# The selected branch's gate moved from the prologue of the last phase into the pair that uses it

## The reference, cut to what matters

```
q, z, gl = split(h @ w_in)                         # z: three gate paths, one per branch
o_cmp = attend(q, 32 compressed keys)
o_sel = attend(q, top-16 blocks of 64 keys)
o_win = attend(q, the last 512 keys)
mix = sum over branches of sigmoid(gl) * o * silu(z)
x = x + gate * (mix @ w_out)
```

## Time and profile before

| | us |
|---|---|
| median of 3 runs | 1825.84 (1825.52 to 1826.37) |
| the profiled execution | 1824.16 |
| its span, first to last instruction | 1822.5 |
| TensorE busy | 1652.4 (91%) |
| VectorE busy | 898.5 (49%) |
| ScalarE busy | 585.5 (32%) |
| GpSimd busy | 500.7 (27%) |

### The profile page before, as it was taken

How to read it: one execution, slowest core, us unless ns; L and a number is a source line. 1 busy time by engine, 2 the same in 40 slices (tenths; PEclk the granted TensorE clock), 3 DMA queues, 4 the chain that set the end, 5 groups by cost and what they waited for, 6 DMA issues and landing times.

```text
span 1822.5 us, 32217 instructions
## 1 busy us (share of the span) xinstructions
PE 1652.4 (91%) x11976; PEld 1464.4 (80%) x11976; DVE 898.5 (49%) x2338; ACT 585.5 (32%) x1310; POOL 500.7 (27%) x305
## 2 busy tenths in 40 slices
PE   3799999996995979789999999999999999998987
PEld 0688888885995977588988888888898888876877
DVE  1444454556226141155555655556555565567345
ACT  2423333432005040023424344243442433434112
POOL 0131322117431332363011110111101111039462
PEclk8899999998998988889999999999999999998998
DMA  9123222333331242301021130211110111133822
GB/s 355 36 93 126 98 100 99 103 130 113 110 117 39 90 143 78 105 24 33 16 59 33 27 79 22 75 33 27 33 27 25 33 27 33 28 96 90 267 84 105
DMA packets 81581, 146.17 MB, mean 80 GB/s; under 512 B 19058, under 2 KB 52882, under 8 KB 81266
## 3 DMA queue, kind: packets, MB, share of 16 engines
q1 hardware_dynamic: 68202, 129.69, 22.1%
q10 hardware_dynamic: 10288, 8.46, 1.5%
q0 software_dynamic: 2944, 6.04, 1.2%
HBM read 130.01 MB, written 19.35 MB: 82 GB/s over the span
## 4 chain that ended last, share of the span: by engine, by line
PE 82%; DVE 7%; ACT 4%; issue 3%; DMA 2%; ACTq 0%; POOL 0%; SPq 0%; DVEq 0%
PE PS L902 15%; PE PS L904 14%; PE PS L903 14%; PE PS L1149 10%; PE PS L1162 9%; PE PS L1129 4%; PE PS L1130 4%; PE PS L1242 3%; ACT XT L1345 2%; ACT HT_r L1348 1%; PE PS L1139 1%; PE PS L1094 1%; PE PS L933 1%; PE PS L1158 1%; DMA KD<-w_bo 1%
## 5 line engine op out<-in xcount | busy, mean ns | idle before, releaser
L902 PE MATMUL PS<-HT_r,WR_r 128*128 128x344 f32 x1368 | 467.5, 342 | 58.6 <-DVE WR L1657 27.6
L904 PE MATMUL PS<-HT_r,WR_r 128*128 128x344 f32 x1368 | 449.3, 328 | 0.0
L903 PE MATMUL PS<-XT_r,WR_r 128*128 128x344 f32 x1368 | 448.7, 328 | 0.0
L594 POOL TENSOR_TENSOR WR_r<-WR,ONE 128x1024 fp32r<-128x1024 f32 x65 | 126.9, 1952 | 1100.9 <-DMA WR<-w_b 650.9
L902 PEld LDWEIGHTS PS<-HT_r,WR_r 128*128 128x128 f32 x1368 | 268.8, 196 | 66.1 <-DVE WR L1657 31.0
L1424 ACT ACTIVATE PB<-PB,NM 128x257 f32<-128x257 f32 (+9 forms) x384 | 249.0, 650 | 178.3 <-DVE NM L1791 178.0
L903 PEld LDWEIGHTS PS<-XT_r,WR_r 128*128 128x128 f32 x1368 | 268.8, 196 | 0.4
L904 PEld LDWEIGHTS PS<-HT_r,WR_r 128*128 128x128 f32 x1368 | 267.7, 196 | 0.0
L1149 PE MATMUL PS<-CST,PB 128*128 128x128 f32 (+1 forms) x1360 | 226.0, 285 | 2.4 <-ACT PB L1420 1.2
L1804 DVE COPY PT<-PS 128x256 f32<-128x256 f32 (+2 forms) x192 | 121.7, 634 | 201.3 <-PE PS L1149 200.5
L1162 PE MATMUL PS<-PT,VT 128*64 128x128 f32 x2592 | 204.0, 285 | 6.5 <-DVE SS L1844 2.8
(11 more groups left out here) (283 smaller groups left out, 2373.1 us busy)
## 6 DMA issues: line engine op xcount, KB each, us to landing
WR<-w_ada SPq DMA_DIRECT2D x64, 512.0 KB, 5.4
WR<-w_b SPq DMA_DIRECT2D x32, 512.0 KB, 3.4
WR<-w_a SPq DMA_DIRECT2D x17, 512.0 KB, 5.0
STR<-scratch SPq DMA_DIRECT2D x128, 48.0 KB, 1.9
KD<-w_bo SPq DMA_DIRECT2D x9, 512.0 KB, 3.7
XT<-x SPq DMA_DIRECT2D x8, 516.0 KB, 15.2
HT<-x SPq DMA_DIRECT2D x8, 516.0 KB, 4.5
x_mid<-HT SPq DMA_DIRECT2D x8, 516.0 KB, 6.1
```

The source lines that it names most:

```text
L594: pool.tensor_tensor(high_r, raw, ONE[:, 0:1].unsqueeze(2).to_broadcast([P, NC, P]), ALU.mult).then_inc(sem("w_split"), 1)
L902: pe.matmul(out, hw[:, k, :], high, start=(k == 0), stop=False)
L903: pe.matmul(out, hw[:, k, :], low, start=False, stop=False)
L904: return pe.matmul(out, lw[:, k, :], high, start=False, stop=(k == NC - 1))
```

## The change

The selected branch's gate leaves the prologue (three thirds fewer there) and is computed in units 0 to 2 of the pair that uses it, where the sliding branch's was. The sliding branch's goes to units 3 to 6, the next pair's queries to units 7 to 10, and the next pair's compressed gate to units 11 to 16. The last pair, which has no next one, now holds six thirds instead of three. The chunks of the weights are numbered and loaded to suit, the query third's last bank is 3 instead of 6, and a wait on an evicted third of the prologue goes.

```diff
-N_Q0, N_AO, N_KV, N_GL, N_B0, N_B, N_BO = 2, 18, 26, 32, 33, 36, 65
+N_Q0, N_AO, N_KV, N_GL, N_B0, N_B, N_BO = 2, 18, 26, 32, 33, 35, 65
...
             prologue.append(third_fill("q", None, 0, a, N_B0 + 1))
-        for a in range(3):
-            prologue.append(third_fill("gate", "sel", 0, a, N_B0 + 2))
         for it in range(PAIRS):
...
-            kinds = [("gate", "win", it, n), ("q", None, it + 1, n + 1), ("gate", "cmp", it + 1, n + 2), ("gate", "sel", it + 1, n + 3)]
+            kinds = [("gate", "sel", it, n), ("gate", "win", it, n + 1), ("q", None, it + 1, n + 2), ("gate", "cmp", it + 1, n + 3)]
             if it == PAIRS - 1:
-                spans = spans[0:3]
+                spans = spans[0:6]
...
-                fl["bank"] = (0, 1, 2, 7)[i] if ph == "a" else (4, 5, 6, 0, 1, 6, 2, 3, 7)[i]
+                fl["bank"] = (0, 1, 2, 7)[i] if ph == "a" else (4, 5, 6, 0, 1, 3)[i]
...
-            weights(N_B0 + 2, t["w_b"][2])
-            weights(N_B, t["w_b"][3])
+            weights(N_B, t["w_b"][2])
+            weights(N_B + 1, t["w_b"][3])
...
-                weights(n + 1, t["w_b"][4 * it + 4])
-                weights(n + 2, t["w_b"][4 * it + 5])
+                weights(n + 2, t["w_b"][4 * it + 4])
+                weights(n + 3, t["w_b"][4 * it + 5])
...
-                weights(n + 3, t["w_b"][4 * it + 6])
...
-                weights(n + 4, t["w_b"][4 * it + 7])
+                weights(n + 4, t["w_b"][4 * it + 6])
...
+                weights(n + 5, t["w_b"][4 * it + 7])
...
-                    pe.wait_ge(*evicted(pl["prologue"][7]))
...
-                    for fl in pl["prologue"][6:9]:
-                        third_out(fl)
```

## The result

| | before | changed |
|---|---|---|
| median of the runs, us | 1825.68 (1818.56 to 1826.37, 4 runs) | 1843.14 (1835.92 to 1847.28, 4 runs) |
| ratio to before, 95% interval | | 1.0101 (1.0072 to 1.0130) |
| the profiled execution, us | 1824.16 | 1839.88 |
| its span, us | 1822.5 | 1838.2 |

The changed kernel is slower by some 18 us (13 to 24 by the interval). The forecast was 1849, with a range of 1832 to 1855. The direction and the larger part of the sum came out as forecast. The first step, on the prologue, did not: there the change gains. The interval is 0.3% to either side, wider than the 0.2% that the prediction allows for.

What follows compares the result with a forecast made beforehand. GpSimd was taken to bound both the prologue's end and the last pair. Start +1.5, closing list +20.5 and clock +1.5 gave +23.5 on 1824.16, 1847.7; against the runs' median the forecast was 1849, range 1832 to 1855.

Steps and rivals of the forecast that it cites:

- The first step: Prologue: taking the gate's thirds off TensorE buys nothing; the start of the pairs' steady part moves by +1.5 us.
- The closing list: Last pair: GpSimd's 66.6 us list begins 24.54 later behind the last third, so the scores come 20.5 us later.
- Rivals 2 and 3: 2: closing list has unseen slack, TensorE's arrival decides, 1837, chance 0.06; 3: GpSimd waited for in neither place, 1820, chance 0.04.
- The clock behind the waits: Behind the waits at the end: TensorE comes out cold, costing +1.5 us, with bounds 0 and 4.4.
- The pairs: Pairs 0 to 6: twelve thirds each at the same units, only rotated, costed at 0.
- rival 4: Pairs: the rotation costs a wait in each of seven pairs, 12.6 us more, 1862; chance 0.05.
- The start of the pairs: Prologue into pair 0: the start of the pairs' steady part moves by +1.5 us.
- the walk turn by turn: Prologue: VectorE's 13 operations alternate one for one with GpSimd's 14, ending at 808.3 against 802.62, before the softmax.
- The prediction's other end for the six copies: Prologue: if the copies into the compressed keys don't wait, VectorE reaches the softmax at 802.6, a move of about -1.
- Rival 1: Prologue: the turns don't bind and the pairs start 15.5 us earlier, the closing list staying late, 1832; chance 0.14.

Runs made afterwards that it cites:

- Run 3: Kernel before, with only GpSimd's closing list made to wait for the softmax of the selected branch's last unit in the last pair: 1.0092 of before, 1843.37 us.
- run 2: Changed kernel with a shorter GpSimd closing list: output and weight splits first, then 20 of 48 value pages, SyncE issuing the other 28: 1.0070 of before.
- run 1: Changed kernel with the split of chunk 36 put ahead of GpSimd's key splits again: 1.0075 of before.
- run 5: Kernel before with the short closing list (output and weight splits first, 20 value pages on GpSimd, 28 on SyncE): 0.9989 of before.
- run 7: Both kernels with short closing list and key splits moved behind the pairs' third and fourth chunks and into pair 1: 0.9963 (before), 1.0020 (changed) of before.

## Why the prediction was right, and where it was not

**The closing list: right, in mechanism and in size.** Rivals 2 and 3, in which nothing waits for the list, are ruled out by the 9.39 and 0.81 that TensorE stood for it. The prediction has 9.9 for the three thirds, 24.54 for the later start of the list, 66.6 for its length and +20.5 for the scores. Measured from the first transpose of pair 7 to the scores: 110.07 less 89.31, +20.8. The thirds cost 10.1 (44.92 less 34.84). The list began 32.70 behind the second transpose of pair 7 (1640.77 less 1608.07) and not 8.17 as before (1620.49 less 1612.32): 24.53 later. Run 3 shows that the lateness of the list alone is enough (ratio 1.0092), run 2 that without it TensorE does not wait.

**The clock behind the waits: too large.** It was put at +1.5 on top. TensorE did come out of the wait slow: the granted clock of the stretch behind it is 0.50, which is 1.2 GHz, and the next is at 2.4 GHz throughout (lengths and busy times as in the earlier trace rows).

```profile
1701.00:1705.40 4.40, 4.36 (x15) 4.39 (x16) 0.00 (x0) 0.00 (x0) 4.38 (x9) 0.50 0.38 107
1705.60:1712.00 6.40, 5.59 (x59) 2.68 (x58) 0.00 (x0) 0.00 (x0) 6.17 (x6) 1.00 0.04 10
```

But this passed while it would have waited for the half split anyway, as one sentence of that step allowed; from the scores to the end nothing was lost (-0.8; the stretch lies between 128.9 and 131.8 in the eleven profiles). Its lower bound, 0, was the answer.

**The pairs: nothing for the rotation, right.** D has the same mean in both orders, to some 4 us with this scatter, and rival 4 (12.6 more) is ruled out by it.

**The start of the pairs: wrong in sign.** The forecast was +1.5, measured -4.4 (B). The step that failed is the walk turn by turn, "one for one they end at 808.3". It laid all of VectorE's 13 operations against GpSimd's 14 and let each wait for a whole one. The trace shows three things that the walk left out.
- The turns are not one for one. A GpSimd operation comes 0.08 behind the last. A VectorE copy of 0.17 that was waiting ends before that, and the next one right behind it begins ahead of GpSimd again: of the four copies at 773.47 two took 0.18, of the two query copies one took 0.17. The longer operations did wait in turn, save one of the four query splits, which took 0.69 because GpSimd was idle then for the 1.03 of chunk 36.
- What waits early costs nothing. The six copies lost 6.7 (8.10 against 1.36 in run 1), but VectorE had idle time after them, until ScalarE had the queries' high parts: 8.91 before, still 3.52 in the changed kernel. The walk added their waits to the path. Of what grew, only the query splits, 4.9 longer, were on it.
- What left had been on the path. Before, the query copies were over at 793.95 and the softmax began at 802.62: the 8.7 between them went to the SiLUs of the three thirds that leave and the copy behind these. In the changed kernel the softmax follows the query copies at once. So the 11.0 that leave TensorE did buy something, 7.3 in B with the key splits where they were (run 1).

Put together, the softmax came 8.4 earlier after the first third than the walk has it, and the way from there to the first transpose took 2.7 longer than its 5.0, because GpSimd, which the walk has idle by then, was not; from the first transpose to the second 11.83 came for 12.0. The two errors partly cancel. The prediction's other end for the six copies (softmax at 802.6, a move of about -1) is not what its own 5.0 and 12.0 give, which is -4.2; that this is near the -4.4 measured is luck, as the softmax was earlier and the way behind it longer. Rival 1, nothing waiting at all, was not what happened either: 4.4 of its 15.5.

The Trainium skill's rule that the prediction drew on (page "SBUF — State Buffer", section "Who interferes with whom") held for the six copies taken together: with GpSimd at work they take 3.75 and 4.35, without it 0.75 and 0.61. It was the way from there to a sum that failed. With the keys behind chunk 36, B is 41.3, and with GpSimd out of the way 36 to 38, so of the 15.5 that the prediction has for nothing waiting, some 12 can be had at the start, though only by moving the key splits and not by this change alone.

**The sum.** Forecast +23.5 on the profiled execution; measured -4.4 (B), +20.8 (E and F), -0.8 (G), and scatter of -3.2 (A) and +3.3 (C and D), which cancel by chance: +15.7. The two terms that were too high, 5.9 at the start and 2.3 of clock, explain why the profiled execution stayed 7.8 below its 1847.7; the median stayed 6 below its 1849.

Open: the gain of the short list on the kernel before in the runs (run 5) is less than in the trace. What lengthens D by up to 8 us between executions of like code is known in part: TensorE's waits in D for the emptied bank at the first units of a pair add up to 20.2 before and to 25.3 in run 5, where it waited 3.9 instead of 2.2 in three of the pairs. Why it does so in some pairs stays open.

## What to carry to other kernels

When work is moved from one end of a phase to the other, look for what is released by its last piece: here a list of 66.6 us hung on the last third, and its lateness cost as much again as the work itself (9.8 came back in run 2; the thirds are 10.1). Before a wait is added to a sum, look whether the waiting engine was idle behind it anyway. And GpSimd's copies between SBUF tiles are best put where VectorE has no short SBUF operations on the path: moving them, and 28 of its 48 page transfers to SyncE, made the kernel before 0.4% faster.

## What the runs showed of the hardware

- A VectorE operation of a quarter of a microsecond can take five to nine times its length beside GpSimd: 128x32 took 1.31 for 0.24, 128x128 took 2.49 for 0.35, 128x14 took 2.10 for 0.23 in the changed kernel. The two longer L1823 of the earlier trace rows, 2.20 and 2.25 there, took 0.69 each in run 7 with the key splits elsewhere. Four such operations wait in the last pair of the kernel before (L1729, L1730, and two behind them, 1.05 and 1.61 for 0.23), and without GpSimd's splits beside them that pair took 74.47 for 83.94, TensorE's higher clock in it included (run 3).
- Operations with one input from PSUM did not wait: three L1654 of 128x344 took 1.36 in the changed kernel while GpSimd was at its key splits, the same as in run 1 without them. Reductions did not either: in the last pair of the changed kernel two of them, 128x14, took 0.17 each, each right ahead of an operation that took 2.10 or 1.62 there and takes 0.23 alone.
